# Linear attention in levels: the fine levels form only diagonal 32x32 blocks, in column groups of the TensorE

## The reference, cut to what matters

```python
rel = cum[:, :, :, None, :] - cum[:, :, None, :, :]
decay = jnp.exp(jnp.where(mask[:, :, None], rel, -jnp.inf))
attn = jnp.einsum('bhid,bhjd,bhijd->bhij', qc, kc, decay)
o = o_inter + jnp.einsum('bhij,bhje->bhie', attn, vc)
...
_, _, og = gla_bidir(qg, kg, vg, gf, gb, s_f, s_b)
```

## Time and profile before

| | us |
|---|---|
| median of 3 runs (2109.69 to 2111.07) | 2110.11 |
| profiled execution, its own time | 2111.35 |
| its span (first to last instruction) | 2109.4 |
| TensorE matmul busy in the span | 2004.8 |
| VectorE, ScalarE, GpSimd busy | 944.7, 746.8, 705.2 |

### The profile page before, as it was taken

How to read it: one execution, slowest core, us unless ns; L and a number is a source line. 1 busy time by engine, 2 the same in 40 slices (tenths; PEclk the granted TensorE clock), 3 DMA queues, 4 the chain that set the end, 5 groups by cost and what they waited for, 6 DMA issues and landing times.

```text
span 2109.4 us, 25505 instructions
## 1 busy us (share of the span) xinstructions
PE 2004.8 (95%) x9924; PEld 1553.6 (74%) x9928; DVE 944.7 (45%) x1358; ACT 746.8 (35%) x1227; POOL 705.2 (33%) x296
## 2 busy tenths in 40 slices
PE   7999988798999999999999999789999999999998
PEld 4787856676888888688888857546876768888885
DVE  2742586935444420544443235666776532222102
ACT  4523365523222221422222134546255432222212
POOL 1321100423444444244444423220421433444442
PEclk9999999889999999999999999899999999999999
DMA  7751110012444442234445422100210222222221
GB/s 303 292 211 41 41 61 1 21 48 102 140 149 149 160 169 89 100 133 147 149 156 192 160 75 80 60 30 21 92 60 31 80 80 81 98 99 93 96 92 58
DMA packets 60126, 223.60 MB, mean 106 GB/s; under 512 B 6800, under 2 KB 7056, under 8 KB 58256
## 3 DMA queue, kind: packets, MB, share of 16 engines
q1 hardware_dynamic: 59472, 220.13, 30.2%
q10 hardware_dynamic: 576, 2.43, 0.3%
HBM read 220.43 MB, written 2.10 MB: 105 GB/s over the span
## 4 chain that ended last, share of the span: by engine, by line
PE 85%; DVE 8%; ACT 3%; issue 2%; DMA 0%; POOL 0%; DVEq 0%; SPq 0%; ACTq 0%
PE ps L430 73%; PE ps L574 3%; DVE hl L649 1%; DVE t L659 1%; DVE neg_max L1159 1%; PE ps L2167 1%; PE ps L1014 1%; ACT w_hi L443 1%; PE ps L2338 1%; PE ps L2359 0%; PE ps L1033 0%; PE ps L2189 0%; PE ps L2329 0%; PE ps L2347 0%; PE ps L936 0%
## 5 line engine op out<-in xcount | busy, mean ns | idle before, releaser
L1784 POOL TENSOR_TENSOR w_lo<-raw,w_hi 128x1024 fp32r<-128x1024 f32 x276 | 665.8, 2413 | 1325.4 <-ACT w_hi L443 723.4
L430 PE MATMUL ps<-hh,w_hi 128*128 128x512 f32 (+1 forms) x1512 | 607.1, 402 | 24.5 <-DVE hl L649 14.8
L430 PE MATMUL ps<-hl,w_hi 128*128 128x512 f32 (+1 forms) x1512 | 597.0, 395 | 0.0
L430 PE MATMUL ps<-hh,w_lo 128*128 128x512 f32 (+1 forms) x1512 | 596.3, 394 | 0.0
L430 PEld LDWEIGHTS ps<-hh,w_hi 128*128 128x128 f32 (+1 forms) x1512 | 287.8, 190 | 104.4 <-issue 32.3
L430 PEld LDWEIGHTS ps<-hh,w_lo 128*128 128x128 f32 (+1 forms) x1512 | 288.0, 191 | 62.9
L430 PEld LDWEIGHTS ps<-hl,w_hi 128*128 128x128 f32 (+1 forms) x1512 | 288.5, 191 | 57.9
L1757 ACT ACTIVATE w_hi<-raw 128x1024 fp32r<-128x1024 f32 x126 | 133.7, 1061 | 472.5 <-PE ps L430 472.5
L496 DVE SCALAR_TENSOR_TENSOR mod_raw<-mod_raw,cond_ada 128x1024 f32<-128x1024 f32 x72 | 119.0, 1655 | 247.3 <-DMA mod_raw<-late 247.3
L430 PE MATMUL ps<-act_hi,w_hi 128*128 (+1 forms) x528 | 209.3, 396 | 0.0
L430 PE MATMUL ps<-act_hi,w_lo 128*128 (+1 forms) x528 | 208.1, 394 | 0.0
(11 more groups left out here) (414 smaller groups left out, 2361.1 us busy)
## 6 DMA issues: line engine op xcount, KB each, us to landing
raw<-stream SPq DMA_DIRECT2D x284, 512.0 KB, 3.4
mod_raw<-late SPq DMA_DIRECT2D x72, 512.0 KB, 4.4
early_raw<-early SPq DMA_DIRECT2D x32, 512.0 KB, 6.5
mod_w<-mod_w SPq DMA_DIRECT2D x8, 1024.0 KB, 19.9
xT<-xT SPq DMA_DIRECT2D x2, 1024.0 KB, 6.5
xT<-xT ACTq DMA_DIRECT2D x2, 1024.0 KB, 6.3
out<-fin SPq DMA_DIRECT2D x8, 256.0 KB, 2.2
csta<-csta SPq DMA_DIRECT2D x1, 1344.0 KB, 5.6
```

What stands on the lines that cost most here:

```text
L430: mm = pe.matmul(out, w, r, start=first and i == 0, stop=last and i == 2)
L1784: pool.tensor_tensor(lo[:, :], raw[n % RING][:, :], hi[:, :].bitcast(F32), ALU.subtract)\
```

## The change

The levels of span 16 and less (li = 3 to 7) and level 0 lie wholly inside the 32x32 blocks on the diagonal. For these, TensorE now forms only those blocks: 64 matmuls of a 64x32 stationary and a 64x32 moving operand, each into its own 32 partitions of PSUM, two banks in place of four. The masked copies of VectorE go into a compact tile `diag` (128 x 512 for all chunks and heads), two instructions of 128x256 in place of four of 128x512. At the end four copies, two on ScalarE and two on VectorE, spread `diag` into `attnT`, and `within` waits for them (`diag_ready`). The mask constants shrink. Level 7 (span 1) no longer decays the keys: its `lk` sums, the exp and the GpSimd multiplication go, and its matmuls read `gkx`. `from_states(0)` moves ahead of level 6 and `from_states(1)` ahead of level 7.

```diff
-for _name, _w in (("rot", 128), ("cos", 512), ("sin", 512), ("carry", 512), ("levels", 128 * (1 + len(LEVELS)))):
+for _name, _w in (("rot", 128), ("cos", 512), ("sin", 512), ("carry", 512), ("fine", 32 * (1 + len(LEVELS) - COARSE))):
...
+    fine_bank = {0: 0, 3: 4, 4: 6, 5: 4, 6: 6, 7: 4}
...
+        if li in fine_bank:
+            for half in range(2):
+                claim(pe, fine_bank[li] + half, ("level", li, half))
+            for u in range(2 * NT):
+                for half in range(2):
+                    rows = slice(64 * half, 64 * half + 64)
+                    for o in range(0, P, 32):
+                        at = (u % 2) * N + (u // 2) * P + o
+                        mm = pe.matmul(ps[o:o + 32, fine_bank[li] + half, u * 32:u * 32 + 32], k[rows, at:at + 32], q[rows, at:at + 32],
+                                       start=True, stop=True)
...
-            if li == len(LEVELS):
+            if li == len(LEVELS) - 1:
                 pe.wait_ge(S("qe_ready"), 2)
                 read(pe, ("u", len(directions) - 1, 4))
                 from_states(0)
+            if li == len(LEVELS):
+                from_states(1)
             pe.wait_ge(S("lq_ready"), li)
-            pe.wait_ge(S("lk_ready"), li)
+            if li < len(LEVELS):
+                pe.wait_ge(S("lk_ready"), li)
             gla_level(pe, li)
-        from_states(1)
-        for b in range(4):
-            read(pe, ("level", len(LEVELS), b))
+        pe.wait_ge(S("diag_ready"), 4)
         within(0)
...
         split_slots(act, firsts["mix1"] + 1)
 
+        read(act, ("level", len(LEVELS), 0))
+        read(act, ("level", len(LEVELS), 1))
+        for o in (0, 32):
+            act.activation(attnT[o:o + 32, :, :, o:o + 32], diag[o:o + 32, :, :, :], ACT.Copy).then_inc(S("diag_ready"), 1)
...
-            for b in range(4):
+            at = 32 * (li - COARSE if li else 0)
+            mask = ca("fine", at, at + 32).unsqueeze(1).unsqueeze(1).broadcast_to([P, NT, 2, 32])
+            for half in range(2):
...
+                got = ps[:, at_bank, 0:2 * NT * 32].rearrange("p (t c i) -> p t c i", t=NT, c=2)
+                to = diag[:, :, half::2, :]
...
-            mark("level_sums", dve.tensor_tensor(to_k[:, :, 0, :], mid_f, fw[:, :, 0, :], ALU.subtract))
-            mark("level_sums", dve.tensor_tensor(to_k[:, :, 1, :], mid_b, bw[:, :, 1, :], ALU.subtract))
+            if s > 1:
+                mark("level_sums", dve.tensor_tensor(to_k[:, :, 0, :], mid_f, fw[:, :, 0, :], ALU.subtract))
+                mark("level_sums", dve.tensor_tensor(to_k[:, :, 1, :], mid_b, bw[:, :, 1, :], ALU.subtract))
...
         attention(len(LEVELS))
+        read(dve, ("level", len(LEVELS), 0))
+        read(dve, ("level", len(LEVELS), 1))
+        for o in (64, 96):
+            dve.tensor_copy(attnT[o:o + 32, :, :, o:o + 32], diag[o:o + 32, :, :, :]).then_inc(S("diag_ready"), 1)
...
-        for li in range(1, len(LEVELS) + 1):
+        for li in range(1, len(LEVELS)):
             pool.wait_ge(S("lk_decay"), li)
             pool.tensor_tensor(lk[li % 2][:, :], lk[li % 2][:, :], k, ALU.mult).then_inc(S("lk_ready"), 1)
```

More of the change, by code:

```diff
@@ L41 @@
 LEVELS = [64, 32, 16, 8, 4, 2, 1]
+COARSE = 2
 GRID_W = 64
@@ L170, in build @@
     vt = sb("vt", [P, NTA, HEADS * DV])
+    region_dn = top[0]
     dn = sb("dn", [32, NALL])
@@ L225, in build @@
     lq = [sb("lq_even", [P, 2 * N]), lq_odd]
+    top[0] = region_dn
+    diag = sb("diag", [P, NT, HEADS, 32])
     top[0] = region
@@ L1240, in halves, with level_done, gla_level @@
         return t.rearrange("p (n two s) -> p n two s", two=2, s=s)
-    def gla_level(pe, li, banks=range(4)):
-        q, k = (lq[li % 2], lk[li % 2]) if li else (gqx[:, :, :].rearrange("p c n -> p (c n)"), gkx[:, :, :].rearrange("p c n -> p (c n)"))
-        for b in banks:
+    fine_bank = {0: 0, 3: 4, 4: 6, 5: 4, 6: 6, 7: 4}
+    def level_done(li):
+        return ("level", li, 1 if li in fine_bank else 3)
+    def gla_level(pe, li):
+        q = lq[li % 2] if li else gqx[:, :, :].rearrange("p c n -> p (c n)")
+        k = lk[li % 2] if 0 < li < len(LEVELS) else gkx[:, :, :].rearrange("p c n -> p (c n)")
+        if li in fine_bank:
[8 more added lines that the diff above has]
+                                       start=True, stop=True)
+                    if u == 2 * NT - 1:
+                        mm.then_inc(bank_full(fine_bank[li] + half), 1)
+            return
+        for b in range(4):
             at_bank = b + 4 * (li % 2)
@@ L1372, in level_decay @@
         def level_decay(li):
+            if li == len(LEVELS):
+                act.wait_ge(S("level_sums"), 4 * (li - 1) + 2)
+                act.activation(lq[li % 2][:, :], lq[li % 2][:, :], ACT.Exp, scale=GATE_SCALE).then_inc(S("lq_decay"), 1)
+                return
             for sums, t, done in ((2, lk[li % 2], "lk_decay"), (4, lq[li % 2], "lq_decay")):
@@ L1380, in blocks @@
                 at_bank = full(act, ("level", li, b))
-                read(act, ("level", li - 1, b))
                 got = ps[:, at_bank, :].rearrange("p (t h i) -> p t h i", t=2, h=2)
@@ L1467, in attention @@
         def attention(li):
-            mask = ca("levels", li * P, (li + 1) * P).unsqueeze(1).unsqueeze(1).broadcast_to([P, 2, 2, P])
-            for b in range(4):
+            at = 32 * (li - COARSE if li else 0)
+            mask = ca("fine", at, at + 32).unsqueeze(1).unsqueeze(1).broadcast_to([P, NT, 2, 32])
+            for half in range(2):
                 if li:
[L1471 to L1474, removed]
+                    read(dve, ("level", li - 1 if li > COARSE + 1 else 0, half))
+                at_bank = full(dve, ("level", li, half))
+                got = ps[:, at_bank, 0:2 * NT * 32].rearrange("p (t c i) -> p t c i", t=NT, c=2)
+                to = diag[:, :, half::2, :]
                 if li == 0:
@@ L1484, in sums @@
             if li >= 3:
-                full(dve, ("level", li - 2, 3))
+                full(dve, level_done(li - 2))
             fw, bw = halves(cumx[:, 0, :], s), halves(cumx[:, 1, :], s)
@@ L2893, in constants @@
     put(first, CSTA, "carry", (t % P != 0)[None, :])
-    levels = [2.0 * np.eye(P)] + [(p[:, None] // (2 * s) == p // (2 * s)) & (p[:, None] // s != p // s) for s in LEVELS]
-    put(first, CSTA, "levels", np.concatenate(levels, axis=1))
+    here = p[:, None] % 32
+    there = np.arange(32)
+    fine = [2.0 * (here == there)] + [(here // (2 * s) == there // (2 * s)) & (here // s != there // s) for s in LEVELS[COARSE:]]
+    put(first, CSTA, "fine", np.concatenate(fine, axis=1))
     return stay, first
```

## The result

The changed kernel took 2099.14 us (median of 6 runs, 2095.31 to 2102.90), the kernel before 2111.13 beside it on the same chip (6 runs, 2109.69 to 2113.62). The ratio is 0.9942, 95% interval 0.9926 to 0.9958. So it is faster by 12 us where 5.6 were forecast, just inside the lower edge of the forecast range (2099). The profiled execution took 2100.49 us with a span of 2098.7.

What follows compares the result with a forecast made beforehand. TensorE bounds most stages; in the levels the VectorE-GpSimd pair sets a 6.0 us period. Tail 4.7 plus level 0 0.9 is 5.6 us, taking 2110.1 to 2104.5; 8-in-10 range 2099 to 2111.

Steps and rivals of the forecast that it cites:

- The period: VectorE's `lq` multiplications stay 6.0 us apart, set by the pair with GpSimd; shorter masked copies gain 0; uncovered, 4.75 us.
- The rule that the prediction cites: A VectorE instruction with two SBUF inputs and a GpSimd instruction reading SBUF exclude each other for the whole instruction.
- The key side of level 7: Two differences (1.2 us) and GpSimd's 2.37 us go; `lq` of level 7 is multiplied 2.5 us earlier.
- A level of small records: TensorE's 128 records a level: 2.5 us at full and 3.0 at half clock, bounds 1.2 and 3.9.
- Rival D: Slower: small records go one after another, 28 ns at full and 57 at half clock; 2120 us; chance 0.13.
- The tail: From level 6 through the spreading copies: `within` starts at 428.9 in place of 433.6, 4.7 us earlier.
- rival B: More: clock full in the tail or up earlier, cheap matmuls, or shorter period; 2 to 7.7 us more; chance 0.17.
- the case of full clock: At full clock `within` starts 6.3 to 7.3 us earlier; copies meet GpSimd's low halves, costing up to 1.2 us.
- the prediction's own sign of being wrong: Among the signs listed as wrong: the four spreading copies before `within` taking over 2 us.
- Rival C: Clock lost later: `within` and the norm behind it at half clock, about 3 to 4 us more; 2108.5; chance 0.23.
- Level 0: TensorE's small matmuls gain 0.3 us and bank 1 is free 0.6 earlier; together 0.9 us.
- Sum: 4.7 + 0.9 = 5.6 us, and 2110.1 - 5.6: Whole kernel: 4.7 us from the tail plus 0.9 from level 0, off the median, giving 2104.5 us.

Runs made afterwards that it cites:

- spread_act: Changed kernel with all four spreading copies on ScalarE; stretch from level 1 to `within` 38.89 us, whole time 2098.29 us (ratio 0.9942).
- undo_key7: Changed kernel, but level 7 decays its keys again; stretch from level 1 to `within` 40.84 us, whole time 2101.59 us (ratio 0.9960).
- keys_on_vector: Changed kernel with the key multiplications of levels 4 to 6 on VectorE instead of GpSimd; stretch 37.67 us, whole time 2096.85 us (ratio 0.9950).
- delay_early_64: Changed kernel with 64 dummy ScalarE activations (6.0 us) ahead of the root of the norm behind the mixer; 6.8 us over layout_only.
- the wider tile: Tile `root_ahead` widened to 64 columns for dummy activations, in six kernels; their profiles lose 0.5 us from 520 to 863 us, 0.6 to 0.7 to 1290.
- The delays: Either kernel with 8 to 64 dummy ScalarE activations ahead of a norm's root; 0.75, 1.5 and 6.0 us cost -0.4, 1.7 and 6.8 against layout_only.
- layout_only: Changed kernel with the wider tile for the dummies and no dummy; 4.1 and 5.6 us slower than the changed kernel (2099.14 and 2097.67).
- delay_a: Changed kernel with 16 dummy ScalarE activations ahead of the root of the norm before ffn2; -0.5 us against layout_only, on another chip.
- delay_early_8: Changed kernel with 8 dummy ScalarE activations (0.75 us) ahead of the root of the norm behind the mixer; -0.4 us against layout_only.
- delay_early_16: Changed kernel with 16 dummy ScalarE activations (1.5 us) ahead of the root of the norm behind the mixer; 1.7 us over layout_only.

## Why the prediction was wrong in its size

**The period: right.** The masked copies of levels 3 to 6 were worth nothing: 0.3 us came out up to level 6, doubling them cost 0.0, and without GpSimd's part the period fell to the 4.75 us forecast. The sum 2.4 + 1.2 + 2.37 = 5.97 is 5.81 here (2.4 + 1.0 + 2.35 and a step), since 1.0 us behind GpSimd's end VectorE begins its next difference. The 5.98 of the kernel before, which the sum seemed to meet, was VectorE's own list with its copies; that the two lay 0.17 apart was chance. The sum also leaves ScalarE out: GpSimd starts when the exp of `lk` is done, and this path (two differences and the exp) is as long as the four differences. Which of the two holds the period, no run separates. The rule that the prediction cites from the Trainium skill ("SBUF — State Buffer", Who interferes with whom) fits all of these runs.

**The key side of level 7: right.** 2.5 us forecast, 2.5 measured between the two multiplications. Undoing it costs only 1.2 at `within`, because GpSimd's low halves end the spread in either kernel, and they start only 1.2 us later.

**A level of small records: mis-sized.** 2.5 or 3.0 us forecast, 1.29 or 1.55 measured, close to the lower bound of 1.2, which came from four weight loads 7 ns apart. I took the middle, and the loads in turn over column groups were the right row. The rule from the Trainium skill, "TensorEngine Tiling (Array Packing)", Instruction Overhead, would have made it 3.2 with 60 cycles for each of the 128 records; the trace does not agree. Counted for each of the 64 matmuls, the estimate from this page of the Trainium skill is 1.6 us at full clock, not far from 1.29, but 3.2 at half, where 1.55 was measured. Rival D fell with it.

**The tail: mis-sized, with two errors against each other.** From the end of the multiplication of level 7 to `within`, 2.2 us were to be gained and 3.9 were. Level 6 and `from_states(1)` took 3.3 us instead of 6.5, since from 416.4 on the clock is full, as in rival B, and the small records are cheap: level 7 began at once and not 3.0 us later. Level 7 itself took 1.94 us with its stop instead of 3.0. Against this, the part behind it took 4.5 us instead of 2.2, because VectorE's two spreading copies took 3.12 us instead of 0.75: the second one alone lasts 2.46 in the chain and ends at 426.07, 0.3 behind GpSimd's low halves (420.96 to 425.79). Such a hold-up was forecast for the case of full clock, as up to 1.2 us; it was 2.4, and with it the prediction's own sign of being wrong, over 2 us for the spreading copies, came true. spread_act removes it and gains only 0.7, since ScalarE's four copies take 2.58.

**Rival C** was right in direction and small in this profile: `within` and what follows did run at 0.69, and cost 0.9 us instead of 3 to 4. But in 3 of the 16 profiles with these levels (undo_key7, keys_on_vector, delay_early_64) the part from `within` to the first projection took 14.3 us at a granted clock of 0.66, 3.2 more than the 10.9 to 11.1 of the kernel before: rival C at its forecast price. In the other 13 it took 11.6 to 12.2.

**Level 0: mis-sized.** 0.9 forecast, 0.7 measured in the first pair, but other profiles differ. In 16 with the same instructions up to there, level 1 starts between 383.84 and 387.70 us, 385.6 on average; in four of the kernel before between 386.88 and 387.64, 387.3 on average. So it is 1.7 us on average. It goes with the clock in part: in spread_act's profile, with the same instructions and a granted clock of 0.88 instead of 0.64 from 344 to 358 us, level 1 starts 2.65 us earlier than in the changed kernel's first profile.

**The step that failed** is the sum itself: "Sum: 4.7 + 0.9 = 5.6 us, and 2110.1 - 5.6". Two things in it are wrong. First, its two terms are too small. The stretch gained 6.7 us, and at 453 us, some 8 us into the first projection, the nine profiles with the changed kernel's levels are 4.0 to 10.3 us ahead of the kernel before, 7.7 on average (6.7 and 8.5 in the two of the changed kernel itself). Second, the sum puts the 1660 us behind at nothing, as one block that moves. They do not move so. Behind 1290 us the granted clock of the same instructions differs from profile to profile (0.68 or 1.00 in one stretch of 10 us). Against the first profile of before, the part behind 453 us was 3.8 and 2.6 us shorter in the two of the changed kernel, and 2.6 to 6.6 in all ten without the wider tile; in three of the kernel before itself it was 0, 0.1 and 4.1 shorter. The run times say the same: they go with the mean clock inside either kernel, and at equal mean clock the gain is 8 to 10 us.

That the median of 2099.14 still fell inside the range, by 0.14 us, was luck. Of rival B, which gave the lower edge, the full clock in the tail and the cheap matmuls came true, and the period was not shortened to 4.75; the part behind 1290 us was in no rival.

What stays open: why the changed kernels come more often with the higher clock behind 1290 us, and whether this would survive another change ahead of it. The delays do not settle it.

## What to carry to other kernels

Before an instruction is shortened, ask what ends the one behind it: here a multiplication on VectorE ended 1.1 us behind GpSimd's, GpSimd's started with the end of ScalarE's exp, and VectorE's copies beside that were all but free. Add up each engine's own list as well as the chain over the engines, since two sums can come to nearly the same period. A long kernel may have stages whose length changes with the granted clock from run to run; profile the kernel before more than once, compare runs at equal mean granted clock, and put the spread between them (here 4 us behind 453 us, and 4 us at level 1) into the range, on either side. When a moved or delayed part is measured by a variant, run its control with the same layout too.

## What the runs showed of the hardware

- Matmuls of 64x32 by 32 columns in f32, in turn over four column groups and two halves of rows, take 12 ns a record at a granted clock of 0.50 and 10 ns at 1.00; with 128 by 128 columns the level took 5.13 and 2.82 us. Small ones hardly feel the clock.
- An f32 copy of 32x512 from SBUF to SBUF on VectorE lasted 0.64 us and then 2.46 beside two GpSimd multiplications, each copy ending 0.28 us behind one of them; with GpSimd done it took 0.42.
- A VectorE multiplication with both inputs in SBUF, started beside GpSimd's of 2.35 us, ended 1.1 us behind it (2.27 us long instead of 1.20); two masked copies, with one input in PSUM, took 0.76 us beside it and 0.77 without.
- The program's time goes with the mean granted clock, 2106.9 us at 0.978 to 0.980 and 2110.7 at 0.973 to 0.974, in one kernel. These runs come from several chips, but on a single one it is the same: 2106.0 to 2107.0 at 0.979 and 2109.6 to 2112.5 at 0.973.
- Widening an unused tile by 252 bytes a partition made the part from 453 to 1290 us 1.3 us longer, in layout_only and, over the delay, in delay_a, delay_early_8 and delay_early_16; 832 more columns in another tile did not. Cause open.
